# Loads ahead of the second attention and of the branch GEMMs, and a batched tail behind the experts

## What is computed

```python
# first block, one layer
gq, gk, gv, nq, nk, nv, fu, cu, gl = split(h @ w_in)       # and the same for 256 context tokens
y_gqa = gqa_latent(q, k, v, kc, vc)                         # 8 heads, 512 + 256 keys
y_na = neighbourhood_latent(nq, nk, nv, nkc, nvc, rpb)      # 8 heads, the same keys, a learned bias
y_fn = fourier_mix(fu)
y_cv = conformer_conv(cu, ...)                              # 31 taps, then a norm and silu
z = einsum('blnc,ncd->blnd', stack(y_gqa, y_na, y_fn, y_cv), w_branch)
x = x + g1 * (sum(sigmoid(gl) * z) @ w_out)
h2 = rms_norm(x, norm2_g) * (1 + sc2) + sh2
x = x + g2 * moe(h2, w_router, router_bias, w_expert_gu, w_expert_down)   # 2 of 16 experts a token
x = rms_norm(x, final_norm_g)
# second block, per layer
h = rms_norm_2(x, attn_norm_w); proj = h @ w_in ...
```

## Time and profile before

| | |
|---|---|
| median of three runs | 3094.94 us |
| profiled execution | 3091.16 us |
| its span | 3089.4 us |
| TensorE, matmuls | 2691.8 us, 87% |
| TensorE, weight loads | 2051.3 us, 66% |
| VectorE | 1830.9 us, 59% |
| ScalarE | 1317.0 us, 43% |
| GpSimd | 160.6 us, 5% |
| mean granted clock of TensorE | 0.938 |

### The profile page before, as it was taken

One profiled execution on the slowest core, in us unless ns is written; L12 is line 12 of the kernel. 1 busy time (PEld: TensorE's weight loads), 2 busy tenths in 40 slices (PEclk: granted clock), 3 DMA queues, 4 the chain that ended last, 5 costly groups with the idle time before them and its releaser, 6 DMA issues.

```text
span 3089.4 us, 32715 instructions
## 1 busy us (share of the span) xinstructions
PE 2691.8 (87%) x11872; PEld 2051.3 (66%) x11872; DVE 1830.9 (59%) x2805; ACT 1317.0 (43%) x1811; POOL 160.6 (5%) x197
## 2 busy tenths in 40 slices
PE   5689989788798399999489979999999997999998
PEld 1468566566576177888376756788878674678886
DVE  5743166577574588999746765544443666644444
ACT  5422256566422177778433245322233315532222
POOL 0011000000000111111100100000000100000000
PEclk9889999999999599999779979999998998999999
DMA  8457224433343189999522442222221234222222
GB/s 315 146 146 217 77 61 123 100 108 92 106 163 123 66 324 364 364 368 354 209 73 75 133 120 72 82 91 87 97 88 64 96 113 128 77 69 95 95 95 75
DMA packets 238009, 436.36 MB, mean 141 GB/s; under 512 B 71568, under 2 KB 94368, under 8 KB 237887
## 3 DMA queue, kind: packets, MB, share of 16 engines
q1 hardware_dynamic: 220335, 391.71, 38.7%
q0 software_dynamic: 17552, 43.05, 4.2%
HBM read 399.84 MB, written 50.58 MB: 146 GB/s over the span
## 4 chain that ended last, share of the span: by engine, by line
PE 65%; DVE 15%; ACT 8%; DMA 5%; issue 4%; POOL 1%; SPq 1%; DVEq 0%; ACTq 0%; POOLq 0%
PE BKP L773 40%; PE BKP L902 3%; PE BKP L945 3%; DMA W<-in_w_expert_gu_dram 2%; PE BKP L1179 2%; PE BKP L1182 2%; PE BKP L1181 2%; PE BKP L1008 1%; DVE WL L2563 1%; PE BKP L843 1%; DVE WL L1899 1%; ACT WH L1698 1%; DMA G<-in_w_expert_gu_dram 1%; PE SCP L878 1%; DVE WL L2053 1%
## 5 line engine op out<-in xcount | busy, mean ns | idle before, releaser
L1899 DVE TENSOR_TENSOR WL<-W,WH 128x2048 fp32r<-128x2048 f32 x131 | 300.2, 2292 | 486.3 <-ACT WH L1326 484.7
L1326 ACT ACTIVATE WH<-W 128x2048 fp32r<-128x2048 f32 x131 | 250.6, 1914 | 630.6 <-PE BKP L773 554.7
L773 PE MATMUL BKP<-hH,WH 128*128 128x512 f32 x896 | 355.1, 396 | 16.2 <-DVE hL L2340 14.1
L773 PE MATMUL BKP<-hL,WH 128*128 128x512 f32 x896 | 350.9, 392 | 0.0
L773 PE MATMUL BKP<-hH,WL 128*128 128x512 f32 x896 | 350.7, 391 | 0.0
L773 PE MATMUL BKP<-WH,aH 128*128 128x512 f32 (+1 forms) x544 | 216.0, 397 | 22.2 <-DVE aL L2543 10.7
L773 PE MATMUL BKP<-WL,aH 128*128 128x512 f32 (+1 forms) x544 | 212.3, 390 | 0.0
L773 PE MATMUL BKP<-WH,aL 128*128 128x512 f32 (+1 forms) x544 | 212.1, 390 | 0.0
L773 PE MATMUL BKP<-WH,hH 128*128 128x512 f32 (+3 forms) x512 | 202.0, 395 | 6.9 <-ACT Z L1377 2.7
L773 PEld LDWEIGHTS BKP<-hH,WH 128*128 128x128 f32 x896 | 170.0, 190 | 56.8 <-issue 18.5
L773 PE MATMUL BKP<-WH,hL 128*128 128x512 f32 (+3 forms) x512 | 194.4, 380 | 0.0
(11 more groups left out here) (474 smaller groups left out, 5751.8 us busy)
## 6 DMA issues: line engine op xcount, KB each, us to landing
W<-in_w_expert_gu_dram SPq DMA_DIRECT2D x46, 1024.0 KB, 7.5
G<-in_w_expert_gu_dram SPq DMA_DIRECT2D x46, 1024.0 KB, 7.8
W<-in_w_in_dram SPq DMA_DIRECT2D x42, 1024.0 KB, 5.5
W<-in_w_up_dram SPq DMA_DIRECT2D x32, 1024.0 KB, 5.2
W<-in_w_down_dram SPq DMA_DIRECT2D x32, 1024.0 KB, 5.0
W<-in_w_expert_down_dram SPq DMA_DIRECT2D x24, 1024.0 KB, 6.7
G<-in_w_expert_down_dram SPq DMA_DIRECT2D x22, 1024.0 KB, 7.0
X<-in_w_in_dram SPq DMA_DIRECT2D x16, 1024.0 KB, 7.5
```

Of the source, the lines that this page charges most:

```text
L773: mm = pe.matmul(BK[j][:, 0:cols], lt, rh, start=start and a == 0, stop=stop and a == len(q) - 1, skip_group_check=True)
L1326: act.activation(WH[s][:], W[s][:], ACT.Copy).then_inc(sems["w_hi"], 1)
L1899: v.tensor_tensor(WL[s][:], W[s][:], WH[s][:].bitcast(F32), ALU.subtract).then_inc(sems["w_lo"], 1)
```

## The change

On SP, the loads of q and k for the second attention's first two heads go into the end of `heads` of the first attention (`next_bias`), behind the last gate units, each behind the `head_lo` of the slot's last head; then both biases; then v, each behind its `head_oe`. The second call of `heads` leaves out its own first loads (`first=False`). Between the two calls the first unit of `w_branch` is loaded into the upper half of `G`; `hi` and `lo` take it from there (`raw`), and its own `unit` call after the second attention goes away.

Behind the experts, ScalarE does the first scaling of each tile (`weighted`), and the squares go into `Y2` in one piece of 1024. VectorE multiplies the joined `X` by `GF1` at once into `XN`, whose squares ScalarE sums as well. Both roots are taken once for all four tiles, the second from the first root and the second sum: with r1 the first root, the second norm's mean is r1 x r1 times the mean square of X times GF1. Then tiles are scaled: `X` by r1 (two tiles on VectorE, two on ScalarE) and `XN` by the product of both roots (four on VectorE).

The diff, without the signature changes and the old lines of the tail:

```diff
@@ SP, heads: at the end
-                T.skip("head_lo", 2)
                 T.skip("head_nm", 2 * NT)
-                sp.wait_ge(sems["head_oe"], T.next("head_oe", 2))
-                sp.sem_inc(sems["paused"], 1)
+                if next_bias is None:
+                    T.skip("head_lo", 2)
+                    sp.wait_ge(sems["head_oe"], T.next("head_oe", 2))
+                    sp.sem_inc(sems["paused"], 1)
+                else:
+                    for s in range(2):
+                        sp.wait_ge(sems["head_lo"], T.next("head_lo"))
+                        sp.sem_inc(sems["paused"], 1)
+                        qk(base + count + s, s)
+                    for s in range(2):
+                        next_bias(s, s)
+                    for s in range(2):
+                        sp.wait_ge(sems["head_oe"], T.next("head_oe"))
+                        sp.sem_inc(sems["paused"], 1)
+                        values(base + count + s, s)
@@ SP, the calls
-            heads(8, 0, KEYS, gates=3840)
             sp.wait_ge(sems["rpb_stored"], T.at("rpb_stored", 16 * 8))
...
-            heads(8, 8, KEYS, na_bias, gates=3840 + 2048)
+            heads(8, 0, KEYS, gates=3840, next_bias=na_bias)
+            load(G[:, 4:8, :], t["w_branch"][0, 0][:, 0:UN].rearrange("(k p) n -> p k n", p=P), f"w_landed{slot[0]}")
+            T.skip("w_lo")
+            slot[0] ^= 1
+            heads(8, 8, KEYS, na_bias, gates=3840 + 2048, first=False)
             load(MC[:, 0:664], t["k_moe"], "moe_landed")
...
-            unit(t["w_branch"][0, 0][:, 0:UN])
             unit(t["w_branch"][0, 0][:, UN:2 * UN])
@@ ScalarE, behind the attentions
-            hi()
+            hi(G[:, 4:8, :])
@@ ScalarE, tail
+            weighted(0)
+            weighted(1)
             for i in range(NT):
...
+                act.wait_ge(sems["x3"], T.next("x3"))
+                act.activation(Y2[:, i, :], X[:, i, :], ACT.Square, scale=1.0 / 32, accum_out=SM[:, 0, i:i + 1]).then_inc(
+                    sems["norm_ss"], 1)
+                if i + 2 < NT:
+                    weighted(i + 2)
+                act.wait_ge(sems["norm_ss"], T.next("norm_ss"))
+                act.wait_ge(sems["x4"], T.next("x4"))
+                act.activation(Y2[:, i, :], XN[:, i, :], ACT.Square, scale=1.0 / 32, accum_out=SM[:, 1, i:i + 1]).then_inc(
+                    sems["norm_ss"], 1)
+                T.skip("norm_ss")
+            act.wait_ge(sems["norm_rd"], T.next("norm_rd"))
+            for i in (2, 3):
+                act.activation(X[:, i, :], XN[:, i, :], ACT.Copy, scale=SM[:, 2, i:i + 1]).then_inc(sems["cb_scaled"], 1)
@@ VectorE, behind the attentions
-            lo()
+            lo(G[:, 4:8, :])
@@ VectorE, tail
             def combined(i):
-                v.wait_ge(sems[f"yc_landed{i}"], 32)
-                link(v.tensor_scalar(XN[:, i, :], XN[:, i, :], GW[:, i, 0:1], None, ALU.mult))
+                v.wait_ge(sems["cb_first"], i + 1)
...
                 v.sem_inc(sems["x3"], 1)
...
+                link(v.tensor_tensor(XN[:, i, :], X[:, i, :], GF1, ALU.mult))
                 v.sem_inc(sems["x4"], 1)
...
+            def roots(y, m, half, work):
+                v.tensor_scalar(half, m, -0.5, None, ALU.mult)
+                link(v.tensor_scalar(y.bitcast(I32), m.bitcast(I32), -0.5, float(0x5F3759DF), ALU.mult, ALU.add))
+                for _ in range(3):
+                    link(v.tensor_tensor(work, y, y, ALU.mult))
+                    link(v.tensor_tensor(work, work, half, ALU.mult))
+                    link(v.scalar_tensor_tensor(y, work, 1.5, y, ALU.add, ALU.mult))
...
+                combined(i)
+            v.wait_ge(sems["norm_ss"], T.next("norm_ss", 2 * NT))
+            r1, both, m, half, work = (SM[:, 2, 0:4], SM[:, 2, 4:8], SM[:, 3, 0:4], SM[:, 3, 4:8], SM[:, 3, 8:12])
+            link(v.tensor_scalar(m, SM[:, 0, 0:4], EPS, None, ALU.add))
+            roots(r1, m, half, work)
+            v.sem_inc(sems["norm_rd"], 1)
+            link(v.tensor_tensor(m, r1, r1, ALU.mult))
+            link(v.tensor_tensor(m, m, SM[:, 1, 0:4], ALU.mult))
+            link(v.tensor_scalar(m, m, EPS, None, ALU.add))
+            roots(both, m, half, work)
+            link(v.tensor_tensor(both, both, r1, ALU.mult))
+            for i in range(NT):
+                if i < 2:
+                    link(v.tensor_scalar(X[:, i, :], XN[:, i, :], SM[:, 2, i:i + 1], None, ALU.mult))
+                else:
+                    v.wait_ge(sems["cb_scaled"], i - 1)
+                v.tensor_scalar(XN[:, i, :], XN[:, i, :], SM[:, 2, 4 + i:5 + i], None, ALU.mult).then_inc(sems["norm_xn"], 1)
+            v.wait_ge(sems["norm_xn"], T.next("norm_xn", NT))
             v.sem_inc(sems["es_free"], 1)
```

More of the change, by code:

```diff
@@ L401, in next_gates, with heads @@
                 gate_unit(u, col)
-            def heads(count, base, nk, bias=None, before=None, gates=None):
+            def heads(count, base, nk, bias=None, before=None, gates=None, first=True, next_bias=None):
                 def qk(h, s):
@@ L412, in values @@
                     load(VS[s][:, 0:nk // P, :], pick(v_d, h)[0:nk, :].rearrange("(t p) d -> p t d", p=P), f"head_landed{s}")
-                for s in range(2):
-                    if before:
-                        before(s)
-                    qk(base + s, s)
-                for s in range(2):
-                    if bias is not None:
-                        bias(s, s)
-                    values(base + s, s)
+                if first:
+                    for s in range(2):
+                        if before:
+                            before(s)
+                        qk(base + s, s)
+                    for s in range(2):
+                        if bias is not None:
+                            bias(s, s)
+                        values(base + s, s)
                 T.skip("head_oe", 2)
@@ L1318, in _, with hi @@
             slot = [0]
-            def hi():
+            def hi(raw=None):
                 s = slot[0]
@@ L1898, in lo @@
                 v.wait_ge(sems["w_hi"], T.next("w_hi"))
-                v.tensor_tensor(WL[s][:], W[s][:], WH[s][:].bitcast(F32), ALU.subtract).then_inc(sems["w_lo"], 1)
+                v.tensor_tensor(WL[s][:], W[s][:] if raw is None else raw, WH[s][:].bitcast(F32), ALU.subtract).then_inc(
+                    sems["w_lo"], 1)
                 T.skip("w_lo")
```

21 lines of the change are left out of this document (5 added, 16 removed).

## The result

The changed kernel took 3074.93 us (median of four runs, 3073.01 to 3077.5) against 3093.54 us for the kernel before beside it: a ratio of 0.9940, 95% interval [0.9923, 0.9957], or 18.6 us. Two more comparisons, of five and six runs on other occasions, gave 0.9932 [0.9919, 0.9946] and 0.9939 [0.9925, 0.9954]; the mean of the three is 0.9937, or 19.5 us. The forecast was 3070.5 with a sum of 23.8 us. So the sign and the places are right, and some 4 us are missing.

The account below looks back on a forecast made before the run. TensorE, busy 87% of the span, was taken to lose time idling at three serial handovers. Gains of 6.3 + 8.4 + 9.1 = 23.8 us gave 3067.4 from the profile or 3071.1 from the median; 3070.5 was taken, range 3063.5 to 3078.

Parts of the forecast that it names:

- Part 1: Between the two attentions: early q, k and bias loads save 5.2 us at ScalarE's start and 1.1 at bias scaling, 6.3 us.
- Part 2: Before the branch GEMMs: weights loaded early into G let TensorE start at 829.2 instead of 837.57, 8.4 us.
- slack of about 3.5 us: Branch stage: the second weight unit is ready at 837.5, while TensorE's first unit lasts to 841.
- Part 3: Behind the experts: ScalarE scaling and batched roots let TensorE restart at 1548.9 against 1557.95, 9.1 us.
- One sign of "wrong": Behind the experts: an idle of VectorE put down to ScalarE would show the forecast wrong.
- Rival 1: Attention handover or branch stage: one prefetch or unit comes late, 6.3 to 8.4 us back, 3077 to 3079; chance 0.09.
- Rival 2: Between the attentions: TensorE's clock stays up at the earlier restart, 2.0 us more gained, 3068.5; chance 0.12.
- Rival 3: Branch stage held at 1.2 GHz after the earlier restart: all 288 matmuls cost 58 us, 3104.5 or so; chance 0.03.
- Rival 4: Behind the experts: ScalarE and VectorE slow each other, 3 us, 3073.5; upper edge of the main case, chance 0.75.
- the three stretches: Between the attentions, before the branch GEMMs and behind the experts: TensorE idles there; gains 6.3, 8.4 and 9.1 us.

Follow-up runs that it names:

- e5: The kernel before the change, nothing edited, profiled once more; the whole run took 3094.46 us.
- e4: Only the change behind the experts (ScalarE scaling, early GF1 product, batched roots), put on the kernel before: ratio 0.9968 to the kernel before.
- e10: Changed kernel with the first branch remainder and hL tile also made before the second attention's last copy: 3064.66 us, ratio 0.9902 to the kernel before.
- e8: Changed kernel with the second attention's first q/k rounding and the first branch remainder also moved under earlier matmuls: 3063.61 us, ratio 0.9905 to the kernel before.
- e3: Only the early load of the first branch weights, issued ahead of the second attention's q and k, on the kernel before: ratio 0.9987.
- e1: The changed kernel again, nothing edited, beside the kernel before: 3072.39 us against 3095.35, ratio 0.9932.
- e9: The changed kernel once more, nothing edited, on one chip with two further kernels: 3076.21 us, ratio 0.9939 to the kernel before.
- e11: Same code as e8, run again beside the changed kernel on one chip: 3061.73 us, ratio 0.9889 to the kernel before.
- e7: Changed kernel with the first scaling of each tile behind the experts back on VectorE: ratio 0.9931 to the kernel before.
- e6: Only the early first branch weights, loaded behind the second attention's first q, k, bias and V, on the kernel before: ratio 0.9972.
- e2: Only the early q, k and bias loads for the second attention, on the kernel before: ratio 0.9979.

## Why the prediction was right, and where it was short

**Part 1, 6.3 us: measured 6.30.** The order of SP came out as worked out. This profile runs 4.2 us late from its opening on; less that, q and k had left by 575.2 and the biases by 582.2, where "before about 580" had been written for all twelve. What was late next was `head_go`, with its memset. ScalarE began 1.29 us behind the copy's start, as forecast (598.65 - 597.37). The bias was scaled as soon as the scores were there. The traffic in the first attention was put at nothing, and it is: that attention lasts 160.0 us in the changed kernel and in e5 with the old loads. It lasts 159.6 to 159.7 us in the three profiles with a first copy before 438 (before, e4, and e10 with the new loads), and 159.9 to 160.1 in the ten others.

**Part 2, 8.4 us: measured 8.16.** `hi` ran at 818.04 under the value matmuls. The 0.2 us are between the copy and `lo`: 1.31 us from start to start, where 0.69 + 0.43 had been counted. The second unit's `lo` was due by 837.5 and ended at 837.74, with the slack of about 3.5 us that e8 then spent: its first product comes 5.2 us sooner after the last copy, and its `lo` 2.1 us sooner, because `y_lo(0)` no longer stands ahead of it there.

**Part 3, 9.1 us: measured 8.91.** The step of 5.33 us, the roots (5.21 us from 1530.62 to 1535.83 for 5.15) and the scalings were right. From the landing of the experts' rows to TensorE's restart the sum has 33.3 us and the trace 33.34 (1506.95 to 1540.29). Small errors cancel in it: ScalarE's scaled copy took 1.15 us and not the 1.05 of the square from which it was taken, and the last square took 1.18 us from its start to the roots for 1.25. What is missing to 9.1 is the landing itself, which came 9.58 us into TensorE's wait and not 9.47. One sign of "wrong" did appear as written, an idle of VectorE put down to ScalarE (5.52 us at 1508.14, 1.33 us at 1530.62); but both waits are terms of the sum, so it was a sign badly chosen and tells nothing against the part.

**Rival 1** didn't occur; e3 shows what it would have been had SP's order been another (4.2 us). **Rival 2** didn't either, for the reason given with the forecast: TensorE restarts at 606.00 at the lower level. Stretches of the changed kernel, with the granted clock behind TensorE's busy time:

```profile
602.00:603.00 1.00, 0.00 (x0) 1.00 0.00 0
603.00:604.00 1.00, 0.00 (x0) 0.85 0.48 104
604.00:605.00 1.00, 0.00 (x0) 0.50 1.06 170
```

The clock fell at about 603.7, 2.1 us behind the last value matmul; in the kernel before it was 4.5 us (601.8 by the earlier trace rows). But the place for it had been put wrongly: the forecast compared the new restart with the old moment of the fall, and that moment moves. The page "TensorE: Matmul & The Clock Gate" of the Trainium skill, in its section on the HAM clock gate, calls the number of slow matmuls at a start variable from run to run. The traces agree: in three profiles of the changed kernel (changed, e1, e9) the clock was back 7.9, 8.5 and 8.6 us behind the restart. The pauses of 0.9 and 1.7 us left the clock up in e8 and e11. The length of a pause alone doesn't decide it, though: a pause of 3.2 us at 412.8 left it up in the profile of before (granted clock 1.00 from 412 to 420), and one of 2.1 us in the second attention was followed by a fall. **Rival 3** (the branch stage at half speed) is out: its first 96 matmuls took 23.40 us, and the granted clock from the first to the last branch product was 0.95 (0.97 before). Its price was added up wrongly: 58 us on top of 3070.5 are 3128, not 3104.5. The row on which it leaned, 1595 to 1600 in the earlier trace rows, is one of matmuls of 72 columns and not of 512. **Rival 4** is out by e7.

**The step that failed is the one behind the sum.** The forecast took everything outside the three stretches to last as before, and so put the rest of the kernel at nothing. By averages of five profiles, the second attention alone took 1.5 us of the gain back. The forecast also worked from one execution.

- *The second attention is longer, by the clock.* Over the five profiles with the old handover 1 or with e3's (before, e5, e4, e3, e6) it takes 214.6 us on average, with 24.0 us at 1.2 GHz; over the five with the change's (changed, e1, e9, e7, e2) 216.1 with 28.9. By these averages 1.5 us are given back. It can't come from the work: all ten have the same matmuls, and e5 with the old code has 216.14. That the new start time makes the long spells likelier is what ten profiles suggest, four of five before and none of five after being under 215.5; it isn't shown to be a rule, and e8 and e11 with one code fall on both sides.
- *The stages were taken from one execution.* The profile of before has the shortest second attention of all thirteen (213.64) and the second shortest opening (437.78); e5 shows the same kernel at 216.14 and 443.02. This accounts for the two profiled spans, which differ by 18.2 us where the three stretches gain 23.4. It doesn't account for the medians of the runs: the forecast of 3070.5 had already been set against the median of 3094.94.

23.4 - 1.5 = 21.9 us lies within all three intervals of the ratio (at 3094 us their lower ends are 23.8, 25.1 and 23.2 us). The parts alone gave 6.5, 8.7 and 9.9 us, 25.1 in all, each known to 3 to 4 us. The 2.4 us between 21.9 and the mean of 19.5 are not assigned. In the same two groups of five profiles the opening, the experts' stage and the layers are 1.2, 1.8 and 1.2 us longer on average with the change's loads. That would be enough, but each is small against the scatter of 6 to 8 us in these stages, so it isn't shown. Part of it may also be that e1 ran at 3069 to 3073 us on one chip and the same code (e9) at 3075 to 3077 on another. In their profiles e9 has 5.8 us more in the layers, with 2.6 us more of TensorE's busy time and 157.6 us at 1.2 GHz for 151.8; what makes up the rest is open.

**What was argued and not tried:** whether a deliberate delay ahead of the second attention would turn the long spells into short ones. The kernels with both handovers show that taking away the pause keeps the clock up at that place, and not surely in the bodies behind it (13.7 us at 1.2 GHz in one profile, 27.3 in the other).

## What to carry to other kernels

Cost a handover by the chain that remains, engine by engine and with the signals between, and the size comes out to a few per cent; what the rest of the kernel does in the meantime needs a range of its own, taken from more than one execution: here single executions of one code differed by up to 13 us on a span of 3090, and the medians of runs by about 4. Here a prefetch was cheap by its place in the issuing queue and not by its size: the same 1 MB load cost 4.2 us ahead of urgent loads and at most 0.4 behind them. After moving loads, look at what still stands between the last matmul of one stage and the first of the next; vector work that depends only on loaded data can go under the last matmuls, which brought the two handovers from 12.1 to 2.7 us here.

## What the runs showed of the hardware

- Where TensorE's clock fell inside the second attention, it came back 3.4 us later in most spells and 6.8 to 6.9 us later in some; before and e4 have one of each at the same place of the same code, and the long one cost 1.6 us. Time at 1.2 GHz in that attention ran from 13.7 to 31.2 us.
- The clock fell 2.1 and 4.5 us behind the last matmul in two profiles of the same stage end, and stayed up over pauses of 0.88, 1.69 and 3.2 us elsewhere.
- ScalarE's copy of 128x1024 with a scale per partition took 1.15 us, its square 1.06 and 0.19 for the accumulator. VectorE's passes lasted 1.28, 1.22 and 1.22 us with and without ScalarE's copies on the same tiles beside them.
- The opening took 437.0 to 443.0 us in thirteen profiles of kernels with the same code there, and TensorE ran at 1.2 GHz for 51.2 to 71.7 us of it, the longer openings with more of it.
